# One of four channel groups of a 31-tap convolution moved from VectorE to GpSimd

## The reference, cut to what matters

```python
def conformer_conv_mixer(a, gate, w_dw, b_dw, ln_g, ln_b):
    u = a * jax.nn.sigmoid(gate)
    u = causal_depthwise_conv(u, w_dw) + b_dw          # 31 taps, 512 channels
    return jax.nn.silu(layer_norm(u, ln_g, ln_b))

def peer_experts(xc, idx, gates, u, v):                # 128 experts a token
    u_sel = jnp.take(u, idx, axis=0)
    act = jax.nn.gelu(jnp.einsum("chkd,cd->chk", u_sel, xc))
    v_sel = jnp.take(v, idx, axis=0)
    return jnp.einsum("chk,chkd->cd", act * gates, v_sel)
```

## Time and profile before

| | |
|---|---|
| median of 3 runs | 2398.9 us (2396.47 to 2402.5) |
| the profiled execution's own time | 2399.6 us |
| its span in the profile | 2397.8 us |
| busy share of the span: PE, DVE, ACT, POOL | 88%, 75%, 49%, 32% |
| mean granted TensorE clock | 0.94 |
| moved by DMA | 777.66 MB, mean 324 GB/s |

### The profile page before, as it was taken

The page is one execution under the profiler, slowest core; times in us unless marked ns, Lnnn a source line. Parts: engine busy times, 40 slices in busy tenths (PEclk is TensorE's granted clock), DMA queues, the critical chain, the costliest instruction groups (busy, mean ns, idle before and its releaser), DMA issues. The chain is left out here.

```text
span 2397.8 us, 28595 instructions
## 1 busy us (share of the span) xinstructions
PE 2120.0 (88%) x9404; PEld 1495.2 (62%) x9404; DVE 1803.4 (75%) x3461; ACT 1165.3 (49%) x3800; POOL 763.1 (32%) x635
## 2 busy tenths in 40 slices
PE   8869998799977778999775688799989999999999
PEld 7545554355532226884343575588459978898997
DVE  6388997858888888988899988766675646656564
ACT  4245555656666665333545654433344435444443
POOL 0124444445455554233465643433310001100000
PEclk9989999899999998999885698899989999999999
DMA  9179998999999999999999999999976544224553
GB/s 378 50 301 409 402 390 341 343 363 417 419 419 421 420 418 355 401 409 420 406 408 364 383 415 421 399 413 421 421 301 207 180 165 145 89 89 158 193 178 140
DMA packets 109764, 777.66 MB, mean 324 GB/s; under 512 B 12320, under 2 KB 13088, under 8 KB 16688
## 3 DMA queue, kind: packets, MB, share of 16 engines
q0 software_dynamic: 73728, 536.90, 55.5%
q1 hardware_dynamic: 35888, 238.93, 25.9%
HBM read 773.69 MB, written 2.10 MB: 324 GB/s over the span
## 5 line engine op out<-in xcount | busy, mean ns | idle before, releaser
L2654 POOL DMA_INDIRECT pair<-in_uv,idx x512 | 642.0, 1254 | 920.2 <-DVE resid L1170 558.2
L1983 ACT ACTIVATE smalls<-smalls 128x1 f32<-128x1 f32 x2060 | 541.1, 287 | 682.8 <-DVE smalls L1837 664.6
L1837 DVE CUSTOM_DVE_ANT_0 pair<-pair,hn 128x1024 f32<-128x1024 f32 x512 | 624.8, 1221 | 152.1 <-DMA pair<-in_uv,idx 150.9
L645 PE MATMUL bank<-pair,diag 128*128 128x512 f32 x884 | 426.2, 611 | 67.2 <-ACT diag L1983 63.7
L645 PE MATMUL bank<-ft,raw 128*128 128x256 f32 x1664 | 374.2, 388 | 11.9 <-DVE ft L1164 11.9
L1170 DVE SCALAR_TENSOR_TENSOR resid<-pair,smalls,resid 128x1024 f32<-128x1024 f32 x286 | 366.5, 1281 | 6.3 <-ACT smalls L1983 6.2
L645 PEld LDWEIGHTS bank<-ft,raw 128*128 128x128 f32 x1664 | 323.6, 195 | 58.4 <-issue 12.7
L645 PEld LDWEIGHTS bank<-pair,diag 128*128 128x128 f32 x884 | 159.7, 192 | 276.6 <-ACT diag L1983 138.1
L1164 DVE TENSOR_TENSOR half<-raw,half 128x1024 fp32r<-128x1024 f32 (+2 forms) x184 | 212.1, 1192 | 122.8 <-ACT half L1983 121.1
L1983 ACT ACTIVATE half<-raw 128x1024 fp32r<-128x1024 f32 (+2 forms) x184 | 179.5, 1023 | 90.9 <-PE bank L645 90.8
L645 PE MATMUL bank<-ft_hi,half 128*128 128x256 f32 x960 | 177.6, 285 | 1.5 <-DVE ft_early L1164 1.5
(11 more groups left out here) (297 smaller groups left out, 3030.3 us busy)
## 6 DMA issues: line engine op xcount, KB each, us to landing
raw<-in_wts SPq DMA_DIRECT2D x201, 1024.0 KB, 8.8
pair<-in_uv,idx POOLq DMA_INDIRECT x512, 11.1
pair<-in_wts SPq DMA_DIRECT2D x7, 1024.0 KB, 13.0
raw<-in_wts SPq DMA_DIRECT2D x10, 512.0 KB, 6.2
wout<-in_wts SPq DMA_DIRECT2D x4, 1024.0 KB, 16.5
raw<-in_wts SPq DMA_DIRECT2D x4, 720.0 KB, 6.5
resid<-in_x SPq DMA_DIRECT2D x4, 512.0 KB, 14.2
out<-resid SPq DMA_DIRECT2D x8, 256.0 KB, 5.7
```

The source lines that it names most:

```text
L645: return e.matmul(o, a, b, start=start, stop=stop)
L1837: e.tensor_tensor_reduce(b[:, 0:1024], b[:, 0:1024], HN[i // 128], 1.0, 0.0, ALU.mult, ALU.add, actv[:, i % 8:i % 8 + 1]).then_inc(dotted, 1)
L1983: return e.activation(o, i, f, **kw)
L2654: e.indirect_dma_start(pair[BUF[i]], None, uv, bass.IndirectOffsetOnAxis(ap=idx[:, n % SLOTS, k:k + 1], axis=0)).then_inc(pairs_in[BUF[i]] ...
```

## The change

The fourth group (channels 384 to 511) leaves VectorE's list, whose pace becomes 1.2 taps a row up to 90. GpSimd makes its 30 taps, one in two rows, at rows 16, 18, ... 74 of its own loop. Each is two instructions: a `tensor_scalar` that writes u times w[j] into a new buffer `ptap` (two of them, 384 columns), and a `tensor_tensor` that adds the buffer to the sum. The second waits for the first and for the sum before. The step stands in front of the wait for the buffer of gather i. TensorE's sum waits for seven groups of `taps_done` and for the 30th tap of GpSimd.

```diff
--- before.py
+++ after.py
@@ -376,6 +376,7 @@
         sq_wide, rt_wide, silu_cf = sem("wide_squared"), sem("wide_root"), sem("cf_silu")
         nrm, y_rs = sem("y_scaled"), sem("y_rate")
         gated_u, copied_z, gained = sem("cf_gate"), sem("sc_value_copied"), sem("y_gained")
+        scaled_tap, pool_tap = sem("tap_scaled_on_pool"), sem("tap_added_on_pool")
         sc_done, tapped = sem("sc_done"), sem("tap_added")
         wout_in = [sem(f"wout_landed{i}") for i in range(4)]
         early_in = [sem(f"early_landed{i}") for i in range(NPAIR)]
@@ -439,6 +440,7 @@
         RSTD = [ar("rstd0", CHAIN + 11776, 128), ar("rstd1", SCORES + 6664, 384)]
         WOUT = [ar(f"wout{i}", a, 2048).rearrange("p (k n) -> p k n", k=4)
                 for i, a in enumerate((SCORES + 2048, SCORES + 6144, SCORES + 4096, CHAIN))]
+        ptap = [ar(f"pool_tap{i}", SCORES + 7168 + 384 * i, 384) for i in range(2)]
         LEAD, SPAN, OUT = (16, 0), (144, 384), (128, 384)
         misc = [MISC]
 
@@ -821,7 +823,8 @@
                         e.wait_ge(gained, 6)
                         y_part(1, "ysc", 3 * h + i, i, ring(("wout", 2 * h, 1), 4), 0)
                 yield 82
-                e.wait_ge(taps_done, 8)
+                e.wait_ge(taps_done, 7)
+                e.wait_ge(pool_tap, 30)
                 colsum(1, "mean", YB[1][:, 4:8])
                 yield 85
                 e.wait_ge(sq_wide, 8)
@@ -1916,7 +1919,7 @@
             for _ in route(0):
                 pass
             u_made(1, 1)
-            other_taps = {at: conv(1, "cf", ct, 9 + ct) for ct, at in enumerate((3, 3.5, 8, 14))}
+            other_taps = {at: conv(1, "cf", ct, 9 + ct) for ct, at in enumerate((3, 3.5, 8))}
             tapped_in = 0
             first, steps = Paced(chain("A")), iter(())
             for n in range(32):
@@ -1937,7 +1940,7 @@
                         if at in other_taps:
                             taps.append(other_taps[at])
                     if taps and i >= 3:
-                        due = min(120, int(1.55 * (i - 2)))
+                        due = min(90, int(1.2 * (i - 2)))
                         pump(due - tapped_in)
                         tapped_in = due
                     if i == HALF + 12:
@@ -2640,13 +2643,29 @@
                 e.tensor_scalar(gat[:, r, :], gat[:, r, :], sm[:, r, 2:3], 0.5, ALU.mult, ALU.mult).then_inc(gated, 1)
 
             e.wait_ge(padded, 4)
-            first, others = Paced(chain("A")), Paced(other_steps())
+            def conv_steps():
+
+                w0, dst = COLS["cf"][0] + 3 * 31, YB[1][:, 7, :]
+                for j in range(1, 31):
+                    yield 14 + 2 * j
+                    if j == 1:
+                        e.wait_ge(first_tap, 12)
+                    if j >= 3:
+                        e.wait_ge(pool_tap, j - 2)
+                    e.tensor_scalar(ptap[j % 2], UP[1][:, 3, j:j + 384], colt[:, w0 + j:w0 + j + 1], None, ALU.mult).then_inc(scaled_tap, 1)
+                    e.wait_ge(scaled_tap, j)
+                    if j > 1:
+                        e.wait_ge(pool_tap, j - 1)
+                    e.tensor_tensor(dst, dst, ptap[j % 2], ALU.add).then_inc(pool_tap, 1)
+
+            first, others, taps = Paced(chain("A")), Paced(other_steps()), Paced(conv_steps())
             for i in range(PAIRS):
                 n, k = divmod(i, 16)
                 first.until(clock(i - 8))
                 if k == 0:
                     e.wait_ge(routed, n + 1)
                 others.until(i - 8)
+                taps.until(i)
                 if WAS[i] is None:
                     chunk_left(e, BUF[i])
                 else:
```

## The result

The changed kernel takes 2408.9 us (median of 5 runs, 2407.0 to 2411.1) against 2397.5 in the same comparison before: ratio 1.0047, 95% interval 1.0034 to 1.0061. It is 11.4 us slower. The profiled execution has a span of 2406.9 us, 9.1 above that of before, whose profiled execution (2399.6 us) was itself 2.1 above the 2397.5.

A forecast was written before the change was run, and what follows sets the result against it. The tap stretch was taken as bound by several engines in turn, closely coupled by seven buffers. Profiled 2399.6 - 0 (removal) + 7.8 (GpSimd's turn) = 2407.4, less 0.7: 2407 us median; forecast range 2403 to 2414, 8 in 10 2389 to 2430.

The forecast's parts named there:

- The bound of the stretch, and the removal: Tap stretch, 180 to 380 us: several engines bind in turn; removing 30 VectorE taps brings 4 to 10 us alone, 0 summed.
- A tap on GpSimd: GpSimd's two added instructions on 384 columns take 3.4 us a tap with gaps, between 1.0 and 4.2.
- GpSimd's turn: Rows 16 to 74: two gathers, gates' share and a tap exceed two rows' 6.25 us by 0.26, costing +7.8 us.
- Signs: Tap stretch: GpSimd busy about 185 us, few waits for TensorE, more VectorE waits for rows, rows 3.25 us, later only shifted.
- VectorE held: GpSimd's 384-column reads delay VectorE by 0 to 36 us; 0 to 18 taken as given back, left out of the sum.
- third rival: Exclusive reads: GpSimd's reads hold VectorE's two-input instructions in the tap stretch; +24 us, 2423 (2416 to 2435), chance 0.20.
- Lumps: GpSimd's waits come in lumps, so a tap could delay catching up; taken to cancel against a full gather queue covering a tap.
- TensorE's changed wait: Channel sum at row 82 waiting for GpSimd's last tap costs 0, with 36 us of cover.

The follow-up runs named there:

- e1_removed: The changed kernel with GpSimd's loop doing no taps, so the fourth group's 30 taps are made by nobody; 2393.3 us.
- e4_narrow: The changed kernel with both GpSimd instructions of a tap on 16 of 384 columns; 2393.1 us.
- e3_writes: The changed kernel with four memsets of 768 columns, reading nothing, in place of each GpSimd tap; 2403.4 us.
- A alone: Theory that GpSimd is occupied and gathers go out late, tested by e3_writes (memsets for taps in the changed kernel); 2403.4 us.
- B alone: Theory that VectorE is held while GpSimd reads, tested by g1_adds_only (one addition a tap in the changed kernel); 2403.0 us.
- f3_short_writes: Against e3_writes, three memsets a tap in place of four; 2395.1 us.
- f5_half_as_many: The changed kernel with a GpSimd tap every four rows, 15 in all, the other 15 made by nobody; 2397.6 us.
- f2_spread: The changed kernel with a tap's multiplication and addition in front of two different gathers, one row apart; 2413.9 us.
- g1_adds_only: The changed kernel with one two-input GpSimd addition of 384 columns a tap, into its own buffer, and no multiplication; 2403.0 us.

## Why the prediction was right, point by point

Forecast 2407 us, measured 2408.9; range and sign hold, the first partly by luck. By steps:

- *The bound of the stretch, and the removal.* 18.4 us less work for VectorE was put at 0 in the sum, 4 to 10 at the most alone. Measured 3.3, so the 4 to 10 were too much for the whole kernel. The reason given, TensorE and transfers at their limit, shows in e1_removed: DMA share 1.00 and VectorE's waits for rows up from 17.2 to 26.4 us.
- *A tap on GpSimd.* 3.4 us predicted, 3.0 measured; its multiplication 1.69 instead of 1.5, its addition 1.18 instead of 1.65. The sum hid two errors. The columns were under-priced: the shortest of the 30 multiplications of 384 columns in the trace takes 1.25 us and the shortest addition 0.99, against 0.33 and 0.22 for 16 columns in e4_narrow, so 2.5 and 2.1 ns a column, not VectorE's 1.04. The waiting behind VectorE was over-priced: 0.84 and 0.69 us (0.71 by its own rows), taken from four of each of the gates' instructions, against 1.69 - 1.25 = 0.44 and 1.18 - 0.99 = 0.19.
- *GpSimd's turn.* Signs: waits for TensorE from 64 us to a few (8.7), rows at 3.25 us (3.29) and the later stretches only shifted are seen; GpSimd is busy 166 us, not 185, and VectorE's waits for rows rise only from 17.2 to 19.3. The price, +7.8, is 10.1 us when measured alone with taps of 3.1 us, but the sum came to it by two errors. With the measured durations the turn is 2 x (1.265 + 0.30) + (0.782 + 0.569 + 0.5) / 8 + 3.0 = 6.36 us, which against the 6.25 of the kernel before gives +3.3. The pace to compare with was wrong too: with the removal alone rows 16 to 80 take 192.2 us, 3.00 each, 6.01 in two, and (6.36 - 6.01) / 2 x 60 = 10.5, near the measured 10.1. Both are estimates from these rows.
- *VectorE held.* The step took 0 to 18 us of it as paid by the 18.4 that were won. It is 20.0: the whole win is given back in kind, and VectorE is as busy as before (181.7 us against 182.0). The forecast said "taps of 384 columns on VectorE still 615 ns"; that is wrong, they are 733. This was the third rival's mechanism. Its price, 36 us of holding and +24 in time, was too high: 20.0 and, alone, +9.0. The rule of the Trainium skill (SBUF — State Buffer, Who interferes with whom), by which a two-input VectorE instruction and a GpSimd instruction that reads wait for each other, is borne out on both sides. By the same section of the Trainium skill VectorE's instructions with at most one SBUF input are spared outside its 2-port performance modes, and `tensor_scalar` can enter these; the 542 and 686 ns above agree with the first, and the short `tensor_scalar` that e3_writes held at 431 ns instead of 171 would fit the second, though no run shows in which mode it was. By the Trainium skill (SBUF — State Buffer, SBUF: two separate sides) the one that is second waits for the whole of the other's instruction. GpSimd's additions agree, after whose end a held tap takes 0.41 to 0.43 us more; its multiplications don't, a held tap ends at least 0.25 us before them, and here the measurement decides.
- *Do the two add up?* By the medians A alone is +10.1 over the removal, B alone +9.0, both together 11.4 + 3.3 = +14.7. The 4.4 us that are missing are within the intervals of the four kernels, 2 to 3 us each. In the profiled executions rows 16 to 80 take 192.2 us with the removal, 203.6 with writes, 201.1 with additions and 210.4 in the changed kernel: 11.4 + 8.9 = 20.3 against 18.2. Whether part of the hold is hidden while VectorE waits for late gathers is open.
- *Lumps* were let cancel against the full queue; f3_short_writes and f5_half_as_many support that, f2_spread doesn't decide it.
- *TensorE's changed wait* at row 82 cost nothing: row 80 is as late (10.0 us) as row 128 (9.8).

So the total came out well partly by luck: two terms left at 0, the removal (-3.3) and the hold (which beside late gathers adds 14.7 - 10.1 = 4.6), nearly cancel, and in the turn a tap that was too long made up for rows that were taken too slow. The mechanism forecast is real; alone it costs as much as the hold alone (10.1 and 9.0), so it isn't the whole.

## What to carry to other kernels

Ask first what the stretch would win if the work simply vanished; here that was 3 us of 18, and an experiment that leaves the work out tells it at once. GpSimd is no free second VectorE: its two-input instructions hold VectorE's two-input instructions. A tap moved from VectorE takes 0.61 us off it, and one addition of 384 columns on GpSimd cost it 0.5 us on average behind a multiplication (14.4 / 30) and 0.7 to 1.0 behind gathers (20.4 / 30 in g1_adds_only, 29.6 / 30 in f2_spread). And an engine that issues the gathers has a turn: sum what it does between two gathers, and set it against the time that the rows would take with the work gone, before adding to it. Here 2.34 us in two rows cost little or nothing, 3.14 us cost 10.

## What the runs showed of the hardware that was not expected

- A one-input multiplication of 384 columns takes GpSimd longer (the shortest 1.25 us) than a two-input addition (0.99, or 0.82 in g1_adds_only, where both inputs are u), but holds VectorE less: 0.31 us against 0.78, and lets go of it at least 0.25 us before its own end.
- GpSimd's writes don't hold VectorE's two-input instructions: four memsets of 768 columns, 0.74 us each, left its tap at 610 ns. They did hold its 16-column `tensor_scalar` with one input, 431 ns instead of 171.
- VectorE's instruction can be lengthened though its record begins first, where GpSimd's addition follows a gather. In g1_adds_only a dot product from 184.17 takes 2.33 us, up to 186.50, beside an addition on GpSimd recorded from 184.57 to 185.41, which wasn't slowed. Spans of GpSimd are rough, so the order isn't certain:

```profile
184.17 2.33 DVE L1840 CUSTOM_DVE_ANT_0 pair<-pair,hn 128x1024 f32<-128x1024 f32 x1 [0.47 <-DMA pair<-in_uv,idx]
```

```profile
184.57 0.84 POOL L2655 TENSOR_TENSOR pool_tap<-u 128x384 f32<-128x384 f32 x1
```
